# The bias of attention is added by TensorE, and maximum and exponentials read PSUM

## The chip, the cores and the metric

The kernel runs on one core of one Trainium2 chip. The metric is device time in microseconds (us), the median of several executions; one further execution is profiled. All data is float32.

## The reference

It is a network on one sequence of 256 tokens and width 1024. Four layers follow each other, each a feed-forward block, an attention block and a feed-forward block; their attention kinds are A, B, C, A. Then come a hybrid block H (attention beside a state-space scan) and a mixture of experts. Cut to what the change touches, each attention computes, per head and block of 128 queries:

```python
s = einsum("bqgrd,bkgd->bgrqk", q, k) * scale + bias      # H: no bias
s = where(ok, s, -1e30)
m = max(s);  m = maximum(m, sink)                         # sink: A only
e = exp(s - m)
denom = sum(e) + exp(sink - m)                            # sink: A only
o = einsum(e / denom, v)
```

The bias is a table of relative distances, one value per head and distance. Head width is 64, so the scale is 1/8. A looks back over a window of 128, B has three branches (compressed keys, selected blocks, window) mixed by gates, C is plain causal attention over the blocks chosen, which at this length are all.

## The kernel before, in words

Feed-forward blocks and projections stream weights through a ring of three slots in SBUF; they aren't touched. Each attention block is a list of units (`units_of`): for each half `a` of the queries (128 tokens) and each quad of four heads one unit, in B three (two scored branches `s` = 0 and 1, then one that only takes the compressed probabilities, `s` = 2). A, C have 8 scored units each, B 16 and 8 compressed ones, H 4. The number of keys `nk` is 128 for the first half of the queries (short units) and 256 for the second (long units); in H it is always 256.

A scored unit goes through these steps, each on one engine, joined by counting semaphores:

- scores, TensorE, L1197: four products over 64 rows into two banks of PSUM. Two pairs of banks are used in turn, by `i % 2`. The products alternate between array rows 0 to 63 and 64 to 127 (`half`).
- the biased pass, VectorE, `biased(i)`, L1283 to L1292: PSUM times 1/8 plus bias (in long units of A two pieces, one from the window table), written to the SBUF tile `scores` or `scores_more`, four of them in turn (`RINGS`). It ends with semaphore `sbias`, which frees the banks: the scores of unit i + 2 wait for it.
- the maximum, VectorE, L1296: a reduction over the SBUF tile, in A two small operations with the sink (L1298, L1300), and the negation L1301, which ends with `smax`.
- the exponentials, ScalarE, L1356: four activations, in place in SBUF, each with the row sum; ends with `sexp`.
- the coefficients, VectorE, L1309 to L1318: two or three small operations, end with `coef`.
- the scaling, GpSimd, L1388: the tile of four heads times the coefficients; ends with `psc`.
- the transposes, TensorE, L1216 (L1211 for a compressed unit): four or eight of 128x128, into banks 4 and 5.
- the copy to SBUF, ScalarE, L1371.
- the values, TensorE, L1237 (L1243 in C, L1233 compressed), and at the end of a query group a copy to `oT` on VectorE, L1322.

Each engine runs its own list in the order written. With `AHEAD = 3` TensorE runs the scores of units 0 to 2, then for each unit `scores(i + 3)`, `transposes(i)`, `values(i - 1)`. VectorE runs `biased` of 0 to 2, then for each unit `coefficients(i)`, `biased(i + 3)`, in H then a part of a convolution (L1698), and the copy out. ScalarE runs the exponentials of 0 and 1, then for each unit those of i + 2 and the copy of i. Before the first attention block the bias tables are put in order by products with a reversed identity (L1431) that ends at `cst[:, C_REV:...]`; after that this region isn't used.

Of the kernel before, what the change touches and what calls it, by code (L numbers as in the profile page):

```python
# [16 lines left out]
ALU = mybir.AluOpType  # L17
# [20 lines left out]
SLOT = 3 * KT * PAIR  # L38
RSQRT_MAGIC = 0x5F3759DF
RINGS = 4  # L40
AHEAD = 3

N_CMP = 15
CMP_STRIDE = 16
# [101 lines left out]
class Semaphores:  # L146


    def __init__(self, nc, ctx):
        def some(names):  # L150
            return [ctx.enter_context(nc.semaphore(n)) for n in names.split()]


        self.raw0, self.raw1, self.raw2, self.slots_used = \
            some("raw0 raw1 raw2 slots_used")

        self.gain0, self.gain1, self.x_in, self.consts_in = \
            some("gain0 gain1 x_in consts_in")

        self.bias_rows_in, self.bias_tab, self.bias_ps, self.bias_sum, self.bias_rows_out, self.bias_in = \  # L160
            some("bias_rows_in bias_tab bias_ps bias_sum bias_rows_out bias_in")
        self.bias_product, self.bias_turned, self.sinks_in = \
            some("bias_product bias_turned sinks_in")

        self.mean_sq, self.power = some("mean_sq power")

        self.ss_done, self.xs_ready, self.tr_done, self.hT_act, self.hT_dve, self.y_done = \
            some("ss_done xs_ready tr_done hT_act hT_dve y_done")
        self.post_used, = some("post_used")

        self.gu_hi, self.dn_hi, self.gu_lo, self.dn_lo, self.gu_done, self.silu = \
            some("gu_hi dn_hi gu_lo dn_lo gu_done silu")
        self.sgc, self.hid_done, self.hid_hi, self.hid_lo, self.down_done = \
            some("sgc hid_done hid_hi hid_lo down_done")

        self.proj, self.evac_act, self.evac_dve = \
            some("proj evac_act evac_dve")

        self.scores, self.sbias, self.smax, self.sexp, self.coef, self.psc = \
            some("scores sbias smax sexp coef psc")  # L180
        self.pT, self.pT_sb, self.oPV, self.oT_sb = \
            some("pT pT_sb oPV oT_sb")

        self.bgate, self.cmp_small, self.z2, self.chid_ps, self.gelu, self.chidT_ps = \
            some("bgate cmp_small z2 chid_ps gelu chidT_ps")
        self.chidT, self.kcb_ps, self.kcb, self.s_cmp, self.cmp_arg, self.cmp_exp = \
            some("chidT kcb_ps kcb s_cmp cmp_arg cmp_exp")
        self.pc, = some("pc")

        self.h_rows, self.h_small, self.h_sq, self.h_rope, self.h_qk_ps, self.h_qT = \  # L190
            some("h_rows h_small h_sq h_rope h_qk_ps h_qT")
        self.h_kT, self.h_ao, self.h_merge1, self.h_conv, self.h_silu, self.h_dtarg = \
            some("h_kT h_ao h_merge1 h_conv h_silu h_dtarg")
        self.h_dtexp, self.h_dta, self.h_acol_ps, self.h_cb_ps, self.h_xt_ps, self.h_row = \
            some("h_dtexp h_dta h_acol_ps h_cb_ps h_xt_ps h_row")
        self.h_arg, self.h_exp, self.h_y, self.h_yss, self.h_yn, self.h_yT_ps = \
            some("h_arg h_exp h_y h_yss h_yn h_yT_ps")
        self.h_yT, self.h_so, self.h_merge2, self.h_mT_ps, self.h_mT, self.h_zs = \
            some("h_yT h_so h_merge2 h_mT_ps h_mT h_zs")
        self.h_w_sum, = some("h_w_sum")  # L200

        self.e_small, self.e_hT, self.e_lg, self.e_arg, self.e_exp, self.e_comb = \
            some("e_small e_hT e_lg e_arg e_exp e_comb")
        self.e_rows, self.e_act, self.comb = \
            some("e_rows e_act comb")

        self.chain_act, self.chain_dve, self.out_done = \
            some("chain_act chain_dve out_done")


class Program:
# [10 lines left out]
    def map_memory(self):  # L222
# [140 lines left out]
        assert self.top <= 229344, self.top  # L363
        self.psum = self.ctx.enter_context(nc.psum_tensor("psum_all", [P, 8, 512], F32))
        self.ident = self.cst[:, C_ID:C_ID + P]
        self.one = self.cst[:, C_ONE:C_ONE + 1]
        self.minus_half = self.cst[:, C_MHALF:C_MHALF + 1]
        self.scratch = nc.dram_tensor("bias_rows", (2, NH, DTOEP), F32, kind="Internal").ap()
# [816 lines left out]
def pe_attention(K, pe, b):  # L1185
# [4 lines left out]
    def scores(i):  # L1190
        x = scored[i]
        if i >= 2:
            pe.wait_ge(K.sem.sbias, S0 + i - 1)
        for t in range(2):
            for half in range(2):
                hs = slice(half * HD, (half + 1) * HD)
                ins = nc.tensor.matmul(K.psum[:, 2 * (i % 2) + half, t * SEQ:t * SEQ + x["nk"]],  # L1197
                                       K.qT[hs, 2 * x["quad"] + t, x["a"] * P:(x["a"] + 1) * P],
                                       K.kT[hs, att.ktile(x["quad"], t, x["s"]), 0:x["nk"]],
                                       start=True, stop=True)  # L1200
        ins.then_inc(K.sem.scores, 1)

    def transposes(x):
# [47 lines left out]
    if kind == "H":  # L1251
        pe.wait_ge(K.sem.h_qT, 1)
        pe.wait_ge(K.sem.h_kT, 1)
    for i in range(AHEAD):
        scores(i)
    for x in b["units"]:
        if x["si"] is not None and x["si"] + AHEAD < len(scored):
            scores(x["si"] + AHEAD)
        transposes(x)
        if x["u"]:  # L1260
            values(b["units"][x["u"] - 1])
# [3 lines left out]
def dve_attention(K, dve, b):  # L1265
# [4 lines left out]
    def head_slice(x):  # L1270
        return slice(4 * x["quad"], 4 * x["quad"] + 4)

    def biased(i):

        x = scored[i]
        nk, hs = x["nk"], head_slice(x)
        src = K.psum[:, 2 * (i % 2):2 * (i % 2) + 2, :].rearrange("p b (h k) -> p (b h) k", h=2)[:, :, 0:nk]
        dst = K.S(i)[:, :, 0:nk]
        dve.wait_ge(K.sem.scores, S0 + i + 1)
        if i >= RINGS:  # L1280
            dve.wait_ge(K.sem.pT, U0 + scored[i - RINGS]["u"] + 1)
        if kind == "H":
            nc.vector.tensor_scalar(dst, src, SCALE, None, ALU.mult).then_inc(K.sem.sbias, 1)  # L1283
        elif kind == "A" and x["a"] == 1:

            nc.vector.scalar_tensor_tensor(out=dst[:, :, 0:P], in0=src[:, :, 0:P], scalar=SCALE,
                                           in1=K.biasA[:, hs, :], op0=ALU.mult, op1=ALU.add)
            nc.vector.scalar_tensor_tensor(out=dst[:, :, P:], in0=src[:, :, P:], scalar=SCALE,
                                           in1=K.bias[:, hs, P:], op0=ALU.mult, op1=ALU.add)\
                .then_inc(K.sem.sbias, 1)  # L1290
        else:
            nc.vector.scalar_tensor_tensor(out=dst, in0=src, scalar=SCALE, in1=K.bias[:, hs, SEQ - nk:],  # L1292
                                           op0=ALU.mult, op1=ALU.add).then_inc(K.sem.sbias, 1)
        dve.wait_ge(K.sem.sbias, S0 + i + 1)
        m = K.am[:, i % RINGS, :]
        K.link(dve, "dve", nc.vector.tensor_reduce(out=m, in_=dst, axis=AX, op=ALU.max))  # L1296
        if kind == "A":
            K.link(dve, "dve", nc.vector.tensor_tensor(m, m, K.sink[:, b["j"], hs], ALU.max))  # L1298

            K.link(dve, "dve", nc.vector.tensor_tensor(K.se[:, i % RINGS, :], K.sink[:, b["j"], hs], m, ALU.subtract))  # L1300
        nc.vector.tensor_scalar(m, m, -1.0, None, ALU.mult).then_inc(K.sem.smax, 1)  # L1301

    def coefficients(i):

# [20 lines left out]

    if kind == "B":
        dve.wait_ge(K.sem.bgate, 1)
    if kind != "H":
        dve.wait_ge(K.sem.bias_turned, len(bias_chunks(K)))
    for i in range(AHEAD):  # L1330
        biased(i)
    for x in b["units"]:
        if x["si"] is not None:
            coefficients(x["si"])
            if x["si"] + AHEAD < len(scored):
                biased(x["si"] + AHEAD)
            if kind == "H":
                dve_conv(K, dve, b, range(2 * x["si"], min(2 * x["si"] + 2, CONV_K)))
        if x["u"] >= 2 and b["units"][x["u"] - 2]["last"]:
# [6 lines left out]
def act_attention(K, act, b):  # L1346
# [4 lines left out]
    def exps(i):  # L1351
        x = scored[i]
        act.wait_ge(K.sem.smax, S0 + i + 1)
        for r in range(4):
            s = K.S(i)[:, r, 0:x["nk"]]
            ins = nc.scalar.activation(s, s, ACT.Exp, bias=K.am[:, i % RINGS, r:r + 1],  # L1356
                                       accum_out=K.den[:, i % RINGS, r:r + 1])
        if kind == "A":
            ins = nc.scalar.activation(K.se[:, i % RINGS, :], K.se[:, i % RINGS, :], ACT.Exp)
        ins.then_inc(K.sem.sexp, 1)  # L1360
# [10 lines left out]
            ins = nc.scalar.activation(K.PT[:, u % 2, 0:nj, :], K.psum[:, 4:4 + nj, :], ACT.Copy)  # L1371
        ins.then_inc(K.sem.pT_sb, 1)

    for i in range(AHEAD - 1):
        exps(i)
    for x in b["units"]:
        if x["si"] is not None and x["si"] + AHEAD - 1 < len(scored):
            exps(x["si"] + AHEAD - 1)
        copy_pT(x)


# [54 lines left out]
def act_bias(K, act, b):  # L1436
    for i, chunk in enumerate(bias_chunks(K)):
        act.wait_ge(K.sem.bias_product, i + 1)
        K.nc.scalar.activation(chunk, K.psum[:, 4 + i % 4, :], ACT.Copy).then_inc(K.sem.bias_turned, 1)


CMP_BANKS = (5, 6, 7, 4)
# [758 lines left out]
```

## Time and profile before

| | us |
|---|---|
| median of 3 runs (3224.70 to 3226.69) | 3224.71 |
| the profiled execution, its own time | 3223.67 |
| its span, first to last instruction | 3221.9 |
| TensorE busy, matmuls | 2902.3 (90%) |
| VectorE busy | 1449.7 (45%) |
| ScalarE busy | 1068.1 (33%) |
| GpSimd busy | 301.4 (9%) |

The page of the profile gives busy time of each engine, the granted clock of TensorE (mean 0.942 of full), and the chain of work that ended last, followed back from the last instruction. The five attention stretches run from the first scores of a block to the first product of its output projection. A product of float32 shows as two records on TensorE, a transpose as one.

### The profile page before, as it was taken

The page shows a single profiled execution, that of the slowest core. Times are in us where ns is not written, and L with a number is a line of the kernel's source. Part 1 is how long each engine was busy: PE and PEld are TensorE (multiplying, and loading weights), DVE is VectorE, ACT ScalarE, POOL GpSimd, SP SyncE. Part 2 cuts the span into 40 slices and gives each one's busy share as a digit, 9 for nine tenths or more (in the row PEclk, how much of TensorE's full clock was granted, in tenths as well). Part 3 has the DMA queues.
Part 4 walks back from the last instruction along what each step waited for, and adds up shares of the span by engine and source line. Part 5 has one row for each costly group of instructions (what it writes and reads, how often), then busy time and mean ns, then how long its engine had stood idle before and what let it go on. Part 6 is the DMA issues. An engine that isn't in the chain of part 4 may idle for free.

```text
span 3221.9 us, 45596 instructions
## 1 busy us (share of the span) xinstructions
PE 2902.3 (90%) x17916; PEld 2489.9 (77%) x17916; DVE 1449.7 (45%) x1815; ACT 1068.1 (33%) x1425; POOL 301.4 (9%) x444
## 2 busy tenths in 40 slices
PE   6988898998878989988898998799895669999999
PEld 5985698997746989975698997399653439999998
DVE  4443445552254454523455552545206525555554
ACT  3334333331163333313333332434103104333333
POOL 0011001001020010001001001100200000000000
PEclk9999999999889999999999999999997779999999
DMA  7532445452404544433454452345331033455442
GB/s 271 195 117 92 161 174 187 170 182 96 170 1 170 195 169 168 171 118 118 170 181 177 164 182 98 138 158 187 105 134 44 27 126 139 175 194 195 173 178 91
DMA packets 330150, 480.06 MB, mean 149 GB/s; under 512 B 9009, under 2 KB 266289, under 8 KB 330081
## 3 DMA queue, kind: packets, MB, share of 16 engines
q1 hardware_dynamic: 320640, 459.73, 40.0%
q0 software_dynamic: 4992, 16.08, 1.5%
q10 hardware_dynamic: 4448, 3.31, 0.3%
q8 instruction: 45, 0.74, 0.1%
q14 instruction: 25, 0.20, 0.0%
HBM read 478.00 MB, written 1.10 MB: 149 GB/s over the span
## 4 chain that ended last, share of the span: by engine, by line
PE 86%; DVE 8%; ACT 2%; POOL 2%; issue 1%; DMA 1%; ACTq 0%; DVEq 0%; PEldq 0%; POOLq 0%
PE psum_all L1030 15%; PE psum_all L1032 14%; PE psum_all L1031 14%; PE psum_all L1044 7%; PE psum_all L1045 7%; PE psum_all L1046 7%; PE psum_all L1091 6%; PE psum_all L1102 5%; PE psum_all L1406 4%; PE psum_all L726 1%; DVE attn_max L1296 1%; PE psum_all L1667 1%; PE psum_all L1216 1%; PE psum_all L1237 1%; PE psum_all L1197 1%
## 5 line engine op out<-in xcount | busy, mean ns | idle before, releaser
L1030 PE MATMUL psum_all<-hT_hi,gu_hi 128*128 128x256 f32 x3840 | 1095.6, 285 | 26.7 <-DVE hT_lo L752 17.2
L1032 PE MATMUL psum_all<-hT_hi,gu_lo 128*128 128x256 f32 x3840 | 1095.7, 285 | 0.0
L1031 PE MATMUL psum_all<-hT_lo,gu_hi 128*128 128x256 f32 x3840 | 1095.5, 285 | 0.0
L1030 PEld LDWEIGHTS psum_all<-hT_hi,gu_hi 128*128 128x128 f32 x3840 | 745.3, 194 | 38.2 <-issue 23.8
L1031 PEld LDWEIGHTS psum_all<-hT_lo,gu_hi 128*128 128x128 f32 x3840 | 745.2, 194 | 8.5
L1032 PEld LDWEIGHTS psum_all<-hT_hi,gu_lo 128*128 128x128 f32 x3840 | 744.9, 194 | 0.0
L841 DVE TENSOR_TENSOR gu_lo<-raw_ring,gu_hi 128x2048 fp32r<-128x2048 f32 x240 | 549.6, 2290 | 59.6 <-ACT gu_hi L829 59.6
L829 ACT ACTIVATE gu_hi<-raw_ring 128x2048 fp32r (+1 forms) x240 | 459.1, 1913 | 6.9 <-DVE oT L1322 6.9
L893 ACT ACTIVATE silu_gate<-psum_all 128x256 f32<-128x256 f32 x240 | 92.1, 384 | 1102.4 <-PE psum_all L1032 1102.4
L1044 PE MATMUL psum_all<-down_hi,hidden_hi 128*128 128x512 f32 x960 | 377.1, 393 | 0.0
L1045 PE MATMUL psum_all<-down_lo,hidden_hi 128*128 128x512 f32 x960 | 376.7, 392 | 0.0
L1046 PE MATMUL psum_all<-down_hi,hidden_lo 128*128 128x512 f32 x960 | 373.9, 390 | 0.0
L948 DVE TENSOR_TENSOR hidden<-silu_gate,psum_all 128x256 f32<-128x256 f32 x240 | 101.2, 422 | 566.4 <-ACT silu_gate L893 564.2
L1007 POOL TENSOR_TENSOR hidden_hi<-hidden,consts_sb 128x256 fp32r<-128x256 f32 x240 | 147.1, 613 | 1945.1 <-DVE hidden L948 1945.1
L836 ACT ACTIVATE down_hi<-raw_ring 128x1024 fp32r (+1 forms) x240 | 254.4, 1060 | 173.3 <-PE psum_all L1046 173.3
L848 DVE TENSOR_TENSOR down_lo<-raw_ring,down_hi 128x1024 fp32r<-128x1024 f32 x240 | 292.6, 1219 | 16.0 <-ACT down_hi L836 16.0
L1091 PE MATMUL psum_all<-hT,raw_ring 128*128 128x256 f32 x896 | 206.1, 392 | 8.5 <-PE psum_all L1091 4.5
L1046 PEld LDWEIGHTS psum_all<-down_hi,hidden_lo 128*128 128x128 f32 x960 | 180.7, 188 | 39.1
L1091 PEld LDWEIGHTS psum_all<-hT,raw_ring 128*128 128x128 f32 x896 | 175.5, 198 | 39.6 <-issue 10.7
L1044 PEld LDWEIGHTS psum_all<-down_hi,hidden_hi 128*128 128x128 f32 x960 | 181.4, 189 | 31.5 <-issue 0.4
L1045 PEld LDWEIGHTS psum_all<-down_lo,hidden_hi 128*128 128x128 f32 x960 | 181.4, 189 | 28.6
L953 DVE TENSOR_TENSOR hidden_lo<-hidden,hidden_hi 128x256 fp32r<-128x256 f32 x240 | 102.1, 425 | 191.3 <-POOL hidden_hi L1007 191.3
(280 smaller groups left out, 1947.6 us busy)
## 6 DMA issues: line engine op xcount, KB each, us to landing
raw_ring<-in_ffn_w_in SPq DMA_DIRECT2D x176, 1024.0 KB, 7.0
raw_ring<-in_w SPq DMA_DIRECT2D x96, 1024.0 KB, 7.4
raw_ring<-in_ffn_w_out SPq DMA_DIRECT2D x88, 1024.0 KB, 9.3
gain<-in_norm_g POOLq DMA_DIRECT2D x24, 512.0 KB, 4.4
raw_ring<-in_c_w_in SPq DMA_DIRECT2D x12, 768.0 KB, 5.2
raw_ring<-in_w_in SPq DMA_DIRECT2D x10, 768.0 KB, 5.8
raw_ring<-in_a_w_in SPq DMA_DIRECT2D x8, 768.0 KB, 5.1
raw_ring<-in_b_w_in SPq DMA_DIRECT2D x8, 768.0 KB, 5.1
```

The costliest lines, as they stand in the source:

```text
L829: K.nc.scalar.activation(K.gu_hi[:, t, :, :], raw_gu(K, slot, t), ACT.Copy).then_inc(K.sem.gu_hi, 1)
L836: K.nc.scalar.activation(K.dn_hi[:, t, :], raw_dn(K, slot, t), ACT.Copy).then_inc(K.sem.dn_hi, 1)
L841: K.nc.vector.tensor_tensor(K.gu_lo[:, t, :, :], raw_gu(K, slot, t), K.gu_hi[:, t, :, :].bitcast(F32), ALU.subtract).then_inc(K.sem.gu_lo, 1)
L848: K.nc.vector.tensor_tensor(K.dn_lo[:, t, :], raw_dn(K, slot, t), K.dn_hi[:, t, :].bitcast(F32), ALU.subtract).then_inc(K.sem.dn_lo, 1)
L1030: nc.tensor.matmul(out, w_hi, K.hT_hi[:, k, :], start=k == 0, stop=False)
L1031: nc.tensor.matmul(out, w_hi, K.hT_lo[:, k, :], start=False, stop=False)
L1032: ins = nc.tensor.matmul(out, w_lo, K.hT_hi[:, k, :], start=False, stop=k == KT - 1)
L1044: nc.tensor.matmul(out, h_hi, d_hi, start=first, stop=False)
L1045: nc.tensor.matmul(out, h_hi, d_lo, start=False, stop=False)
L1046: ins = nc.tensor.matmul(out, h_lo, d_hi, start=False, stop=last)
L1091: ins = nc.tensor.matmul(K.psum[:, bank, 0:SEQ], w[:, k, it["c0"]:it["c0"] + P], K.hT[:, k, :], start=k == 0, stop=k == KT - 1)
L1102: ins = nc.tensor.matmul(K.psum[:, bank, 0:it["n"]], K.hT[:, k, a * P:(a + 1) * P], w[:, k, it["c0"]:it["c0"] + it["n"]], start=k == 0 and ...
```

## The change

The biased pass goes. The scaled identity 8 x I is made once by a ScalarE copy over the reversed identity (semaphore `eight_id`). TensorE adds the bias as the first product of each bank's accumulation, 8 x I times the bias table, and the scores accumulate on it, so that PSUM holds the unscaled scores plus 8 x bias. The products are ordered by half: bias (two pieces in long units of A), then the two score products of this half. The maximum reduces PSUM; in A the scale comes in the operation with the sink, else in the negation. The exponentials read PSUM, with the scale as the activation's factor, and write the SBUF tile. The banks are now free when the exponentials have ended: scores wait for `sexp`. Work is issued two units ahead, and VectorE runs `maxima(i + 2)` before `coefficients(i)`. H has no bias product.

```diff
 def scores(i):
         x = scored[i]
         if i >= 2:
-            pe.wait_ge(K.sem.sbias, S0 + i - 1)
-        for t in range(2):
-            for half in range(2):
-                hs = slice(half * HD, (half + 1) * HD)
-                ins = nc.tensor.matmul(K.psum[:, 2 * (i % 2) + half, t * SEQ:t * SEQ + x["nk"]],
+            pe.wait_ge(K.sem.sexp, S0 + i - 1)
+        nk = x["nk"]
+        for half in range(2):
+            hs = slice(half * HD, (half + 1) * HD)
+            bank = K.psum[:, 2 * (i % 2) + half, :].rearrange("p (t k) -> p t k", t=2)
+            h0 = 4 * x["quad"] + 2 * half
+            if kind == "A" and x["a"] == 1:
+                nc.tensor.matmul(bank[:, :, 0:P], K.eight, K.biasA[:, h0:h0 + 2, :], start=True, stop=False)
+                nc.tensor.matmul(bank[:, :, P:], K.eight, K.bias[:, h0:h0 + 2, P:], start=False, stop=False)
+            elif kind != "H":
+                nc.tensor.matmul(bank[:, :, 0:nk], K.eight, K.bias[:, h0:h0 + 2, SEQ - nk:], start=True, stop=False)
+            for t in range(2):
+                ins = nc.tensor.matmul(bank[:, t, 0:nk],
                                        K.qT[hs, 2 * x["quad"] + t, x["a"] * P:(x["a"] + 1) * P],
-                                       K.kT[hs, att.ktile(x["quad"], t, x["s"]), 0:x["nk"]],
-                                       start=True, stop=True)
+                                       K.kT[hs, att.ktile(x["quad"], t, x["s"]), 0:nk],
+                                       start=kind == "H", stop=kind == "H" or t == 1)
...
-    for i in range(AHEAD):
+    if kind != "H":
+        pe.wait_ge(K.sem.eight_id, 1)
+    for i in range(2):
         scores(i)
     for x in b["units"]:
-        if x["si"] is not None and x["si"] + AHEAD < len(scored):
-            scores(x["si"] + AHEAD)
+        if x["si"] is not None and x["si"] + 2 < len(scored):
+            scores(x["si"] + 2)
         transposes(x)
...
-        dst = K.S(i)[:, :, 0:nk]
         dve.wait_ge(K.sem.scores, S0 + i + 1)
-        if i >= RINGS:
-            dve.wait_ge(K.sem.pT, U0 + scored[i - RINGS]["u"] + 1)
...
-            nc.vector.scalar_tensor_tensor(out=dst, in0=src, scalar=SCALE, in1=K.bias[:, hs, SEQ - nk:],
-                                           op0=ALU.mult, op1=ALU.add).then_inc(K.sem.sbias, 1)
-        dve.wait_ge(K.sem.sbias, S0 + i + 1)
         m = K.am[:, i % RINGS, :]
-        K.link(dve, "dve", nc.vector.tensor_reduce(out=m, in_=dst, axis=AX, op=ALU.max))
+        K.link(dve, "dve", nc.vector.tensor_reduce(out=m, in_=src, axis=AX, op=ALU.max))
...
-    for i in range(AHEAD):
-        biased(i)
+    for i in range(2):
+        maxima(i)
     for x in b["units"]:
         if x["si"] is not None:
+            if x["si"] + 2 < len(scored):
+                maxima(x["si"] + 2)
             coefficients(x["si"])
-            if x["si"] + AHEAD < len(scored):
-                biased(x["si"] + AHEAD)
...
         act.wait_ge(K.sem.smax, S0 + i + 1)
+        if i >= RINGS:
+            act.wait_ge(K.sem.pT, U0 + scored[i - RINGS]["u"] + 1)
         for r in range(4):
-            s = K.S(i)[:, r, 0:x["nk"]]
-            ins = nc.scalar.activation(s, s, ACT.Exp, bias=K.am[:, i % RINGS, r:r + 1],
-                                       accum_out=K.den[:, i % RINGS, r:r + 1])
+            nk = x["nk"]
+            src = K.psum[:, 2 * (i % 2) + r // 2, (r % 2) * SEQ:(r % 2) * SEQ + nk]
+            ins = nc.scalar.activation(K.S(i)[:, r, 0:nk], src, ACT.Exp, bias=K.am[:, i % RINGS, r:r + 1],
+                                       scale=SCALE, accum_out=K.den[:, i % RINGS, r:r + 1])
...
+    K.nc.scalar.activation(K.eight, K.ident, ACT.Copy, scale=1.0 / SCALE).then_inc(K.sem.eight_id, 1)
```

## Rows read from the trace of the kernel before

**Rows 1.** The page: the chain that ended last, shares by engine.
```profile
PE 86%; DVE 8%; ACT 2%; POOL 2%; issue 1%; DMA 1%; ACTq 0%; DVEq 0%; PEldq 0%; POOLq 0%
```

**Rows 2.** Table by stretch (A, B, C, A, H): length, busy (instructions), clock, DMA share, GB/s.
```profile
287.12:326.55 39.43, 24.29 (x161) 14.88 (x161) 26.27 (x76) 23.17 (x82) 11.72 (x8) 0.83 0.00 1
883.42:962.33 78.91, 60.73 (x385) 35.82 (x385) 45.22 (x104) 46.12 (x153) 23.44 (x16) 0.81 0.00 1
1496.56:1531.38 34.82, 23.61 (x208) 17.87 (x208) 22.17 (x48) 20.95 (x73) 11.73 (x8) 0.90 0.25 92
2016.09:2053.73 37.64, 22.63 (x160) 13.91 (x160) 26.80 (x76) 23.16 (x82) 11.72 (x8) 0.91 0.24 84
2448.43:2487.72 39.29, 21.52 (x96) 14.29 (x96) 33.58 (x69) 15.79 (x43) 8.01 (x4) 0.60 0.00 0
```

**Rows 3.** The chain in order of time, block B: start, us, engine, tile, line.
```profile
935.51 1.90 POOL scores_more L1388
...
937.46 1.97 PE psum_all L1216 x8
939.43 1.71 PE psum_all L1237 x8
941.14 0.54 PE psum_all L1211 x4
941.68 1.02 PE psum_all L1237 x8
942.70 1.09 PE psum_all L1197 x8
...
943.81 1.24 DVE scores_more L1292
...
945.07 1.23 DVE attn_max L1296
...
947.06 1.90 POOL scores L1388
```

**Rows 4.** Timeline of the first A: start, us, engine, line, operation, tiles [idle <-releaser].
```profile
288.69 0.69 DVE L1296 TENSOR_REDUCE attn_max<-scores 128x4 f32<-128x512 f32 x1
...
302.32 1.04 POOL L1388 TENSOR_TENSOR scores_more<-scores_more,attn_coef 128x512 f32<-128x512 f32 x1 [4.55 <-DVE attn_coef L1318]
...
303.47 1.22 DVE L1296 TENSOR_REDUCE attn_max<-scores 128x4 f32<-128x1024 f32 x1
...
307.33 1.22 DVE L1296 TENSOR_REDUCE attn_max<-scores_more 128x4 f32<-128x1024 f32 x1
...
308.97 0.17 DVE L1301 TENSOR_SCALAR attn_max<-attn_max 128x4 f32<-128x4 f32 x1
...
309.69 0.49 ACT L1356 ACTIVATE scores_more<-scores_more,attn_max 128x256 f32<-128x256 f32 x1
```

**Rows 5.** Groups by line, biased passes: busy us, mean ns | idle before, releaser.
```profile
L1292 DVE SCALAR_TENSOR_TENSOR scores<-psum_all,bias_full 128x512 f32<-128x512 f32 (+1 forms) x16 | 14.2, 888 | 31.6 <-PE psum_all L1197 31.5
...
L1286 DVE SCALAR_TENSOR_TENSOR scores<-psum_all,bias_window 128x512 f32<-128x512 f32 x4 | 2.7, 683 | 3.9 <-PE psum_all L1197 3.9
```

**Rows 6.** TensorE prices: two lines of the chain, then four of the timeline.
```profile
275.87 10.58 PE psum_all L1431 x24
...
789.10 14.07 PE psum_all L1091 x64
...
303.42 0.66 PE L1216 MATMUL psum_all<-consts_sb,scores_more 128*128 128x128 f32 x4 [2.33 <-POOL scores_more L1388]
304.00 0.65 PE L1237 MATMUL psum_all<-probsT,v_tok 128*64 128x256 f32 x4
...
942.63 1.14 PE L1197 MATMUL psum_all<-kT,qT 64*128 64x256 f32 x8
943.70 1.09 PE L1216 MATMUL psum_all<-consts_sb,scores 128*128 128x128 f32 x8
```

**Rows 7.** The chain in order of time, block H: a part of the convolution.
```profile
2465.79 6.36 DVE h_xbcT L1698 x12
```

**Rows 8.** Timeline, first A: the scores of the first long unit.
```profile
296.50 2.08 PE L1197 MATMUL psum_all<-kT,qT 64*128 64x256 f32 x8
```

More of the change, by code:

```diff
@@ L40 @@
 RINGS = 4
-AHEAD = 3
 N_CMP = 15
@@ L177, in __init__ @@
             some("proj evac_act evac_dve")
-        self.scores, self.sbias, self.smax, self.sexp, self.coef, self.psc = \
-            some("scores sbias smax sexp coef psc")
+        self.scores, self.eight_id, self.smax, self.sexp, self.coef, self.psc = \
+            some("scores eight_id smax sexp coef psc")
         self.pT, self.pT_sb, self.oPV, self.oT_sb = \
@@ L365, in map_memory @@
         self.ident = self.cst[:, C_ID:C_ID + P]
+        self.eight = self.cst[:, C_REV:C_REV + P]
         self.one = self.cst[:, C_ONE:C_ONE + 1]
@@ L1271, in head_slice, with maxima @@
         return slice(4 * x["quad"], 4 * x["quad"] + 4)
-    def biased(i):
+    def maxima(i):
         x = scored[i]
@@ L1277, in biased @@
         src = K.psum[:, 2 * (i % 2):2 * (i % 2) + 2, :].rearrange("p b (h k) -> p (b h) k", h=2)[:, :, 0:nk]
-        dst = K.S(i)[:, :, 0:nk]
         dve.wait_ge(K.sem.scores, S0 + i + 1)
-        if i >= RINGS:
-            dve.wait_ge(K.sem.pT, U0 + scored[i - RINGS]["u"] + 1)
[L1282 to L1291, printed above, removed]
-            nc.vector.scalar_tensor_tensor(out=dst, in0=src, scalar=SCALE, in1=K.bias[:, hs, SEQ - nk:],
-                                           op0=ALU.mult, op1=ALU.add).then_inc(K.sem.sbias, 1)
-        dve.wait_ge(K.sem.sbias, S0 + i + 1)
         m = K.am[:, i % RINGS, :]
-        K.link(dve, "dve", nc.vector.tensor_reduce(out=m, in_=dst, axis=AX, op=ALU.max))
+        K.link(dve, "dve", nc.vector.tensor_reduce(out=m, in_=src, axis=AX, op=ALU.max))
         if kind == "A":
-            K.link(dve, "dve", nc.vector.tensor_tensor(m, m, K.sink[:, b["j"], hs], ALU.max))
+            K.link(dve, "dve", nc.vector.scalar_tensor_tensor(out=m, in0=m, scalar=SCALE, in1=K.sink[:, b["j"], hs],
+                                                              op0=ALU.mult, op1=ALU.max))
             K.link(dve, "dve", nc.vector.tensor_tensor(K.se[:, i % RINGS, :], K.sink[:, b["j"], hs], m, ALU.subtract))
-        nc.vector.tensor_scalar(m, m, -1.0, None, ALU.mult).then_inc(K.sem.smax, 1)
+        nc.vector.tensor_scalar(m, m, -1.0 if kind == "A" else -SCALE, None, ALU.mult).then_inc(K.sem.smax, 1)
     def coefficients(i):
@@ L1327, in dve_attention @@
         dve.wait_ge(K.sem.bgate, 1)
-    if kind != "H":
-        dve.wait_ge(K.sem.bias_turned, len(bias_chunks(K)))
-    for i in range(AHEAD):
-        biased(i)
+    for i in range(2):
+        maxima(i)
     for x in b["units"]:
         if x["si"] is not None:
+            if x["si"] + 2 < len(scored):
+                maxima(x["si"] + 2)
             coefficients(x["si"])
-            if x["si"] + AHEAD < len(scored):
-                biased(x["si"] + AHEAD)
             if kind == "H":
@@ L1372, in copy_pT @@
         ins.then_inc(K.sem.pT_sb, 1)
-    for i in range(AHEAD - 1):
+    for i in range(2):
         exps(i)
     for x in b["units"]:
-        if x["si"] is not None and x["si"] + AHEAD - 1 < len(scored):
-            exps(x["si"] + AHEAD - 1)
+        if x["si"] is not None and x["si"] + 2 < len(scored):
+            exps(x["si"] + 2)
         copy_pT(x)
```

## The prediction

> **What bounds the kernel now.** I read first the chain of work that ended last: TensorE is 86% of it, VectorE 8% [rows 1]. The table by stretch then gives the five attention stretches, which are all that the change touches: 230.1 us together, with TensorE busy for 152.8, VectorE for 154.0, ScalarE for 129.2 and GpSimd for 66.6 [rows 2]. No engine fills them; they are bound by a chain from engine to engine, and the question is which links it has after the change. Call a unit's steps S (scores), b (the biased pass), M (maximum and its small operations), E (exponentials), C (coefficients), G (GpSimd's scaling), T (transposes) and V (values). In block B the chain goes round once per pair of scored units: G 1.90, T 1.97, V 1.71, the transposes of the compressed unit 0.54, V 1.02, S 1.09, b 1.24, M 1.43, C 0.66, in all 11.55 us from G to G [rows 3]. So GpSimd's scaling is in the loop already, because TensorE's queue runs S(i+3) ahead of T(i), but behind T(i-1). In A, VectorE sets the pace of the long units: one long reduction starts 3.86 us after the one before [rows 4].
>
> **Removed.** The b passes: two groups of 14.2 and 14.1 us, four of 2.7 and two of 2.4, 43.9 us of VectorE [rows 5] (one row stands there for the two first groups, one for the four of 2.7). It is the most that can be saved.
>
> **Moved, and this is the point on which I forecast.** Work was issued three units ahead, now two. TensorE's queue is S0, S1, then S(i+2), T(i), V(i-1) for each unit; VectorE's is M0, M1, then M(i+2) before C(i). Follow it: M(k) must end before C(k-2) starts; then G(k-2), then T(k-2), V(k-3), and only behind these, in TensorE's order, S(k+1), which M(k+1) waits for. Every maximum thus hangs on the one before by C, G, T, V, S and M in series: one round per unit, where before there was one per pair. The new wait of S(i) for the exponentials of i-2 comes due earlier than the wait behind T (E of a long unit is 4 x 0.49 + 0.19 = 2.2 us [rows 4], while C, G and T take 3.7), so it costs only at a block's start. The wait for pT in front of the exponentials looks four units back and costs nothing. The number of maximum-to-maximum rounds beyond the first three maxima is 5 in each A, 5 in C, 13 in B.
>
> **S itself.** Before, the two halves of the array work side by side: a long S takes 1.14 [rows 6]. Now each half is: bias product over all 128 rows, then two products on 64 rows, then the same for the other half; the full-array product between them separates the halves. A 512-column f32 record takes 10.58/24 = 0.44 and each product has two; a 256-column one 14.07/64 = 0.22; eight 128-column records take 1.09, less a tail of 0.2, so 0.11 each [rows 6]. Long: 4 x 0.43 + 8 x 0.215 = 3.45; short: 4 x 0.22 + 8 x 0.11 = 1.73. Going from one shape of the array to another costs some 0.2: the S of 942.63 needs four pairs of records, 0.87, and the next T starts after 1.07 [rows 6]. Three such changes more, 0.6, and a tail of 0.16 give 4.2 and 2.5. Bounds: 3.4 with no change costing anything, 4.8 with 0.4 for each. The Trainium skill, "TensorEngine Tiling (Array Packing)", Key Properties, says that changing the tiling mode drains the engine; it gives no time. The 0.2 agrees with it, and the rule speaks against this change; the sum rests on the row.
>
> **The other links.** M: long in A, from 307.33 to the end of the last small operation at 309.14, 1.82 [rows 4]; in B and C 1.43 [rows 3]; short 0.53 less, as the short reduction takes 0.69 against 1.22 [rows 4]. The reduction now reads PSUM: b, which read the same 1024 elements out of PSUM, took 1.24 [rows 3], so I add nothing (0 to 0.1 each). C: three small operations in A and B, two in C and H, at 0.2 each like those of M, so 0.58 and 0.38. G with its two hand-overs: 2.0 long, 1.15 short [rows 3, 4]. T and V long take 1.05 and 1.02, start to start [rows 3, 6], short 0.58 each (T's start to V's [rows 6], V taken to be the same). The exponentials out of PSUM lie beside this chain (0 to 0.1 each way). The scaled identity is one ScalarE copy, 0.2 once.
>
> **Sum, with TensorE at its full clock.** A round in A: short 6.7; short with a long S and M behind it 8.9; long 0.57 + 2.0 + 1.05 + 1.02 + 4.2 + 1.85 = 10.7. A from the first S: M2 ends at 9.6 (S0 2.7, M0 1.3, E0 1.75, S2 2.5, M2 1.3), then 6.1, 8.9, 8.9, 8.9, 10.3, so the last maximum ends at 52.8; then a tail of 11.9 (C5, G5, T5, V4, a copy, C7, G7, T7, copy, V7, copy). In all 64.7, against 39.4 and 37.6 [rows 2]: +25.3 and +27.1. C: M2 ends at 8.4, then 5.5, 8.4, 8.4, 8.4, 9.8, a tail of 12.4 (its V has sixteen records of half the length, and I give it 0.5 more): 61.2 against 34.8: +26.4. B has two kinds of round. Out of a first unit: C, G, T, the compressed V 0.5, S, M: 9.8 long, 6.2 short. Out of a second one T must be copied (1.1) before the compressed transposes (0.54) and V can go: 12.0 long, 7.6 short. With 8.4 at the start, 27.6 for two short pairs, 6.2 + 9.85 + 8.45 + 9.85 across the change of length, 2 x 21.8, 9.8 and a tail of 13.5: 137.3 against 78.9: +58.4. H has no bias, its queue of VectorE is full of convolution (rounds of 6.36 us) [rows 7], and S stays at 1.1. It loses its four b, 4.8, and gains a stall in front of M2, which waits for E0 2.2 and S2 1.2 while M1 takes 1.43: 2.0. So H gives -2.8. Together +134.4 us.
>
> **TensorE's clock.** Right after G, with TensorE idle before it, T came at half clock (1.97 for eight records against 1.09 behind S), V in part (1.71 against 1.02), and a long S once (2.08 against 1.14) [rows 3, 6, 8]; the granted clock of the attention stretches is 0.81 to 0.91 but for H's 0.60 [rows 2]. Now TensorE stands idle in each round for M, C and G, 4.4 us if long and 2.7 to 3.0 if short, longer than before the T at 937.46, whose G alone took 1.9. T and V at half cost 0.9 and up to 0.9 more; the head of S sometimes comes with them. I take 2.0 per round: 28 x 2.0 = 56. The tails of before had such stretches in them and mine don't: 4 x 1.5 = 6; B begins behind long vector work, so its first S at half: 2.5. Together +64.5. Bounds: 0, and all of TensorE's work in these rounds at half, about +134. The Trainium skill, "TensorE: Matmul & The Clock Gate", HAM oscillation, says that idle gaps between bursts of matmuls bring the clock down and each burst then starts slow; the rows agree.
>
> 3223.7 (the profiled execution; its span 3221.9; the median of the runs is 1.0 higher) + 134.4 + 64.5 = 3422.6, so 3423. DMA and the feed-forward blocks keep their times: in the first A and in B the DMA share during attention is 0.00, so a longer stretch there delays no transfer and hides none [rows 2].
>
> **Rivals.** (1) The rounds as above, but TensorE is not slowed: its S, now longer, keeps the clock up: 3223.7 + 134.4 = 3358. For it: T behind S took 1.09 [rows 6]. Against: T behind G took 1.97 [rows 3], and in the new order T is always behind G. (2) The clock stays at half through nearly all: 3223.7 + 134.4 + 134 = 3492; H does so already, at 0.60 [rows 2]. (3) S is cheap, since the halves still overlap and the bias record of one half slips beside the products of the other: S 2.2 and 1.4 instead of 4.2 and 2.5: 28 rounds at 1.6 less, and about half as much again where they would have run at half clock, 68 in all: 3355. (4) Faster: VectorE is the bound as in A's 3.86 us, and the loop over G doesn't close. Then the 43.9 us of b go and the pace of a long unit is that of ScalarE, whose 2.2 us of E and about 1.0 of copy lie under the 3.86 of today: 3223.7 - 43.9 = 3180. It decides if S(k+1) can be worked before T(k-2) ends; TensorE's queue is in order and T stands before it, and B's chain goes through G today, so this needs my reading of the order to be wrong. (5) The two effects cancel and nothing can be measured: 3224.
>
> **How the numbers follow.** My case 0.70, between 3370 and 3475; (1) 0.09, (2) 0.11, (3) 0.05, (4) 0.03, (5) 0.02. The likeliest gives 3423. The range 3355 to 3485 takes in my case, (1) and (3) and leaves out (2), (4) and (5), 0.16. Faster by over 0.2% (about what a measurement of this kernel can tell from no change) 0.03, within 0.2% 0.02, slower 0.95.
>
> **What would show it.** In the chain of waits of the changed kernel, B must show C, G, T, V, S, M once per unit and no b; the starts of long reductions in A should be 10.7 us apart or more, in B about 10 and 12 in turn. A long S should span near 4 us at full clock. Stretches: A 76, B 167, C 73, H 37. VectorE's busy time should be 44 us lower and its idle time far higher, waiting for the scores. TensorE's granted clock should be lower in A, B and C. It would be wrong if starts of reductions lie closer than E + S + M, or if T comes at full clock after each G.

## The result, and the profile after

The changed kernel takes 3443.8 us (median, 3440.5 to 3445.4), the kernel before 3225.3; the ratio is 1.0675, 95% interval 1.0657 to 1.0694. The profiled execution has a span of 3440.6 us, 218.7 more than before. From the page of the changed kernel, the engines, then the chain that ended last:

```profile
PE 3067.4 (89%) x18108; PEld 2574.9 (75%) x18108; DVE 1411.4 (41%) x1763; ACT 1064.2 (31%) x1426; POOL 301.4 (9%) x444
...
PE 87%; DVE 7%; POOL 2%; ACT 2%; DMA 1%; issue 1%; SPq 0%; DVEq 0%; PEldq 0%; ACTq 0%
```

The table by stretch of the changed kernel, bounds as in [rows 2] (A, B, C, A, H): length, busy time of TensorE, its weight loads, VectorE, ScalarE, GpSimd, then granted clock, DMA share, GB/s.

```profile
290.33:367.97 77.64, 53.86 (x208) 32.80 (x208) 19.40 (x64) 22.25 (x81) 11.72 (x8) 0.76 0.00 0
924.51:1109.13 184.62, 137.74 (x448) 71.14 (x448) 30.56 (x88) 45.13 (x152) 23.44 (x16) 0.63 0.00 0
1643.42:1715.03 71.61, 52.91 (x240) 32.81 (x240) 15.54 (x41) 20.22 (x72) 11.72 (x8) 0.81 0.12 45
2200.46:2276.03 75.57, 51.78 (x208) 31.79 (x208) 19.42 (x64) 22.32 (x82) 11.72 (x8) 0.80 0.12 42
2670.49:2707.51 37.02, 20.54 (x96) 14.23 (x96) 30.46 (x65) 14.04 (x40) 8.01 (x4) 0.71 0.00 1
```

The five lengths sum to 446.5 us against 230.1: +216.4, so all but 2 us of the loss is here. VectorE is busy 38.7 us less (115.4 against 154.0), as meant. TensorE is busy for 164 us more, and in A, B and C its clock is lower (in H it is higher, 0.71 for 0.60). The two largest groups of S in the changed kernel: bias products (L1203; those of A's long units, L1200 and L1201, stand apart) and score products (L1205), busy us, mean ns, and idle time before them.

```profile
L1205 PE MATMUL psum_all<-kT,qT 64*128 64x256 f32 (+1 forms) x352 | 100.4, 439 | 3.6 <-DVE kT L1641 1.9 <-ACT scores L1352 1.7
L1203 PE MATMUL psum_all<-bias_full,consts_sb 128*128 128x256 f32 (+1 forms) x128 | 75.0, 678 | 8.7 <-DVE cmp_probs L1504 5.6 <-ACT consts_sb L1436 1.0 <-ACT attn_sink_exp L1355 1.0
```

And the group that waits: before its 44 maxima VectorE stood idle for 303.6 us, waiting for the scores. Before the change it was the biased passes that waited for them, 48.2 us in all their groups together, 31.6 of them in the group of [rows 5].

```profile
L1290 DVE TENSOR_REDUCE attn_max<-psum_all 128x4 f32<-128x1024 f32 (+1 forms) x44 | 43.2, 982 | 303.6 <-PE psum_all L1205 303.6
```

The chain in order of time through a query group of long units in B, which answers to [rows 3]: start, us, engine, tile, line (L1384 is GpSimd's scaling, L1224 transposes, L1241 and L1245 values, L1219 compressed transposes, L1290 the maximum).

```profile
1042.29 0.96 PE psum_all L1219 x4
1043.26 1.10 PE psum_all L1245 x8
1044.35 1.06 PE psum_all L1203 x2
1045.41 1.06 PE psum_all L1205 x4
1046.47 1.05 PE psum_all L1203 x2
1047.52 1.07 PE psum_all L1205 x4
...
1048.62 1.24 DVE attn_max L1290
...
1050.61 1.90 POOL scores_more L1384
...
1052.56 1.97 PE psum_all L1224 x8
1054.53 1.05 PE psum_all L1241 x4
1055.58 2.01 PE psum_all L1203 x2
1057.58 2.00 PE psum_all L1205 x4
1059.59 2.00 PE psum_all L1203 x2
1061.59 2.02 PE psum_all L1205 x4
...
1063.63 1.24 DVE attn_max L1290
...
1065.62 1.90 POOL scores_more L1384
```

Two things can be seen. The chain goes round once per scored unit, from G at 1050.61 to G at 1065.62, 15.0 us; in [rows 3] it was 11.55 for two units. And S takes 4.24 us the first time (four pieces of 1.06) and 8.03 the second (four of 2.0): the same instructions at full and at half clock (2.4 and 1.2 GHz).

### The profile page after: what moved, and what is told of

Read it like the earlier page. It is cut to its first block, busy times and chain, and to the rows that moved or that the text cites. A ratio compares the mean times of both kernels' runs of the same rounds, so it can differ in the third digit from the quotient of the medians.

```text
span 3440.6 us, 45928 instructions
## 1 busy us (share of the span) xinstructions
PE 3067.4 (89%) x18108; PEld 2574.9 (75%) x18108; DVE 1411.4 (41%) x1763; ACT 1064.2 (31%) x1426; POOL 301.4 (9%) x444
## 4 chain that ended last, share of the span: by engine, by line
PE 87%; DVE 7%; POOL 2%; ACT 2%; DMA 1%; issue 1%; SPq 0%; DVEq 0%; PEldq 0%; ACTq 0%
PE psum_all L1030 14%; PE psum_all L1031 14%; PE psum_all L1032 14%; PE psum_all L1044 6%; PE psum_all L1045 6%; PE psum_all L1046 6%; PE psum_all L1091 6%; PE psum_all L1102 4%; PE psum_all L1402 4%; PE psum_all L1205 3%; PE psum_all L1203 2%; PE psum_all L1224 2%; PE psum_all L726 1%; DVE attn_max L1290 1%; PE psum_all L1245 1%
## 5 line engine op out<-in xcount | busy, mean ns | idle before, releaser
L1046 PEld LDWEIGHTS psum_all<-down_hi,hidden_lo 128*128 128x128 f32 x960 | 180.3, 188 | 39.3
```

Source lines behind the costliest of these rows:

```text
L1046: ins = nc.tensor.matmul(out, h_lo, d_hi, start=False, stop=last)
```

## The experiments

Three causes had to be told apart: the order and the number of units ahead; the bias products with their longer S; and the clock. The times are those of each kernel against the kernel before on the same chip (3224.4 to 3225.3).

**The order alone, put into the kernel before.** Bias and scores stay as they were.

```diff
-AHEAD = 3
+AHEAD = 2
...
-            coefficients(x["si"])
             if x["si"] + AHEAD < len(scored):
                 biased(x["si"] + AHEAD)
+            coefficients(x["si"])
```

(ScalarE's exponentials keep their two units ahead.)

> The kernel before with nothing but the order of the change: two units ahead on TensorE and VectorE, the biased pass and maximum of unit i + 2 in front of the coefficients of unit i. Bias stays on VectorE, scores stay short. Theory (the order alone closes the loop once per unit): as the changed kernel without bias products (3331) plus the biased pass in 28 rounds, 1.25 us long or 0.7 short, so 3355 to 3370, with A near 62 and B near 139. Rival (the order only hurts together with banks held until the exponentials end): within 20 us of 3225.

Measured 3362.3 us, ratio 1.043 (1.0413 to 1.0448). Its two first stretches, A and B:

```profile
287.36:350.27 62.91, 30.17 (x160) 18.33 (x160) 26.91 (x76) 23.65 (x82) 11.72 (x8) 0.67 0.00 0
907.29:1045.59 138.30, 75.90 (x384) 43.87 (x384) 45.56 (x105) 47.22 (x152) 23.44 (x16) 0.63 0.00 0
```

62.9 and 138.3, where 62 and 139 were expected. The order and the units ahead cost 137 us by themselves. This is shown, and the rival, that it only hurts with banks held longer, is out. Part of the 137 is clock: it is 0.67 and 0.63 here, where [rows 2] has 0.83 and 0.81. The two, one unit less ahead and the maximum before the coefficients, were not tried apart in this kernel; in the changed one, the second alone is worth 131 us (two kernels further down).

**The changed kernel without bias products.** Bias and mask are left out; the scores are those of the kernel before.

> The changed kernel without the bias products, so bias and mask are left out; the score products alternate between the halves as before the change. It tells the price of the bias on TensorE from that of the order. Theory of the prediction: 20 long rounds lose 3.06 us each and 8 short ones 1.8, 75 us, and with the half clock some 110, so about 3335, which leaves some 110 us over the kernel before to the order alone. Rival (the bias products are all of it): within 20 us of 3225.

Measured 3331.4, ratio 1.033 (1.0312 to 1.0349): near the 3335 expected. So the loss splits, by edits and with what each does to the clock: order and units ahead +137.0 (3225.3 to 3362.3), the biased pass gone from it -30.9 (3362.3 to 3331.4), the bias products and the order of the halves +112.4 (3331.4 to 3443.8). The middle figure also holds the change to banks freed by the exponentials. VectorE's saving is thus real, 31 of its 44 us, and it is bought with 112.

**The changed kernel with the old order on VectorE.** Two units ahead stay, as do the bias products.

```diff
+            coefficients(x["si"])
             if x["si"] + 2 < len(scored):
                 maxima(x["si"] + 2)
-            coefficients(x["si"])
```

> The changed kernel, but VectorE runs the coefficients of unit i before the maximum of unit i + 2. Theory (the order closes a loop once per unit): coefficients and GpSimd's scaling no longer wait for the maximum of two units later, the loop goes round once per two units, and TensorE's own work of 6.3 us per long and 3.7 us per short unit sets the pace. Attention stretches near 50 (A), 100 (B), 50 (C), 37 (H) instead of 78, 185, 72, 37, so about 3280 in all. Rival (the longer scores on TensorE are the cause, the order hardly matters): the time stays within 30 us of 3444.

Measured 3313.2, ratio 1.0276 (1.0257 to 1.0294): 131 us back for two calls exchanged. The expectation of 3280 was 33 too low: B alone took 49 us more than expected, the others a little less. Its A, B and C, and then a part of its B by itself:

```profile
287.99:334.29 46.30, 41.59 (x208) 25.97 (x208) 18.31 (x64) 21.70 (x82) 11.74 (x8) 0.96 0.00 0
891.20:1039.98 148.78, 137.59 (x448) 70.53 (x448) 28.08 (x88) 43.68 (x152) 23.46 (x16) 0.62 0.00 1
1575.93:1621.70 45.77, 43.12 (x240) 27.45 (x240) 14.52 (x41) 19.60 (x72) 11.74 (x8) 0.96 0.20 70
...
937.00:985.00 48.00, 45.20 (x110) 20.30 (x108) 8.38 (x27) 12.82 (x47) 6.91 (x5) 0.50 0.00 1
```

A and C took 46 where I expected 50. In those 48.0 us of B TensorE was busy for 45.2 and had half its clock all the time. The clock is low at the start of B, where TensorE has waited for VectorE's long work, but hardly a gap is left that could keep it there: another reason was wanted, and the next three kernels look for it. The low clock did end in this block, at about 999.5, behind a stretch in which TensorE had run transposes and values and no scores (start, us, engine, tile, line):

```profile
997.09 1.91 PE psum_all L1245 x8
999.00 1.54 PE psum_all L1203 x2
1000.54 1.06 PE psum_all L1205 x4
```

**The changed kernel with the halves side by side again.** Both bias products first, then the score products alternating.

```diff
-            for t in range(2):
-                ins = nc.tensor.matmul(bank[:, t, 0:nk],
+        for t in range(2):
+            for half in range(2):
...
+                ins = nc.tensor.matmul(banks[half][:, t, 0:nk],
```

> The changed kernel, but both bias products of a unit come first and then the four score products, alternating between the two halves of the array as before the change. Work and idle gap of a round stay, the scores of a long unit should take 2.95 instead of 4.2 us, of a short one 1.6 instead of 2.5 (at full clock). By that alone 28 rounds are 1.1 us shorter, about -31 us, to 3413. Theory on the clock (products that fill only half the array's rows let the clock fall or stay low): the granted clock in B rises from 0.63 to over 0.70 and the gain is 50 to 80 us. Rival on the clock (only TensorE's idle share counts): less work beside the same idle gap, so the clock in B is no higher than 0.63 and the gain is at most 45 us.

> The kernel with the halves alternating and the order of the change once more, for its profile: 3392 us was measured for it, 51 less than the changed kernel. Theory (half-filled products keep the clock low): the granted clock in B is over 0.70 against 0.63 of the changed kernel. Rival (idle share only): 0.63 or lower, and the gain comes from the shorter scores at half clock.

Measured 3392.3, ratio 1.0513 (1.0495 to 1.0532), 51 us less than the changed kernel, and 3393.2 in a single further run, from which this row of B comes:

```profile
916.16:1071.26 155.10, 108.10 (x448) 56.45 (x448) 30.40 (x89) 45.20 (x152) 23.43 (x16) 0.72 0.00 1
```

TensorE has less to do in each round beside the same idle gap, and yet its clock is higher, 0.72 against 0.63. The idle share alone doesn't explain this. In the other blocks it went the other way: the clock was 0.73 in the first A (0.76 in the changed kernel), 0.79 in C (0.81) and 0.77 in the second A (0.80), as the rival on the clock would have it. And in B, too, an S behind T and V still ran at half clock as a whole, 3.71 and 1.83 us where the next one took 1.91 and 1.09:

```profile
999.32 3.71 PE psum_all L1203 x4
1003.03 1.83 PE psum_all L1207 x8
...
1015.23 1.91 PE psum_all L1203 x4
1017.14 1.09 PE psum_all L1207 x8
```

**Both edits.**

> Both edits at once: VectorE runs coefficients before the maximum, and the score products alternate between the halves behind the two bias products. The kernel with the order alone took 3313, with its B stretch at 148.8 us and a granted clock of 0.62 although TensorE was busy for 137.6 of them. Theory on the clock (score products on half the array at a time don't bring a low clock back up): with the halves side by side the clock in B comes to over 0.85, TensorE needs 5.0 us per long unit and 2.8 per short one, stretches 42, 90, 42, 42, 37 and 3240 to 3250 in all. Rival (the clock in B stays low for another reason, as the block begins at half clock): clock in B at 0.65 or lower, B near 125, the whole near 3280.

Measured 3250.3, ratio 1.0079 (1.0062 to 1.0096). Its A and B:

```profile
288.71:328.94 40.23, 33.40 (x208) 22.20 (x208) 18.49 (x64) 21.59 (x81) 11.72 (x8) 0.96 0.00 0
885.42:983.14 97.72, 80.21 (x448) 43.81 (x448) 28.19 (x88) 43.66 (x152) 23.45 (x16) 0.92 0.00 1
```

B goes from 148.8 to 97.7 us by the order of each unit's products alone, its clock from 0.62 to 0.92. The block begins at half clock here too, so that isn't enough to hold it down. The edit does two things at once: it puts the two bias products one behind the other, and it alternates the halves. Which of them lets the clock come back was not tried.

**A warmed start of B.** The kernel with only VectorE's order undone (3313), with eight useless full-array products of 512 columns on TensorE while it waits before the first scores of B.

> The kernel with the order alone undone, and eight useless full-array products of 512 columns on TensorE while it waits before the first scores of B, nothing else. In that kernel B began at half clock and stayed there (0.62, 148.8 us) while A and C, which begin at full clock, kept 0.96 with the same products. Theory (score products on half the array keep a full clock but don't bring back a low one, so it is how the block starts): B stays near full clock, over 0.85, takes 98 to 110 us, and the whole about 3265 to 3275. Rival (something in B itself, its compressed units or their waits, holds the clock down): B stays above 140 us and the whole near 3313.

Measured 3282.2, ratio 1.018 (1.0165 to 1.0196), and B:

```profile
895.43:1006.11 110.68, 94.00 (x450) 49.74 (x448) 28.23 (x88) 43.76 (x153) 23.47 (x16) 0.95 0.00 1
```

The same instructions take 110.7 us instead of 148.8 when the block starts at full clock: the rival, something in B itself, is out. The stretch is at the upper end of the expectation and the whole 7 us above it, in part because B now begins about 4 us later (895.43 for 891.20), behind the useless products. With the run before, this is what the rows show: in the order bias, half, bias, half a full clock is mostly kept, and a low one lasts long, even with hardly a gap. It is no rule without exceptions. In the kernel with VectorE's order undone the clock came back at about 999.5, and in the first A of the changed kernel it came back in the middle of an S, at about 350.4. The eight products ahead of B had it back before the first S. What decides it in each case stays open.

Nor is it the order of the halves that keeps them apart. In H of the changed kernel the halves are written one after the other as well, but with no bias product between them, and the eight records take the 1.14 us of [rows 6]:

```profile
2676.19 1.14 PE L1205 MATMUL psum_all<-kT,qT 64*128 64x256 f32 x8 [1.65 <-ACT scores L1352]
```

So what separates the halves in A, B and C is the full-array product between them, as the prediction had it.

**The idle gap filled.** The changed kernel with useless full-array products between the scores of unit i + 2 and the wait for the scaled probabilities of unit i. They write bank 4, so the wait that frees it (`pT_sb`) now stands before them.

```diff
...
+            if kind != "H" and x["si"] + 2 < len(scored):
+                for _ in range(3 if x["nk"] == SEQ else 2):
+                    nc.tensor.matmul(K.psum[:, 4, :], K.ident, K.bias[:, 0:2, :].rearrange("p h s -> p (h s)"),
+                                     start=True, stop=True)
             pe.wait_ge(K.sem.psc, S0 + x["si"] + 1)
```

> The changed kernel with useless full-array products on TensorE between the scores of unit i + 2 and the wait for the scaled probabilities of unit i: three of 512 columns (2.6 us at full clock) in long units, two in short ones, in the time in which TensorE otherwise idles. Nothing that is needed waits for them at full clock. Theory (the idle gap of each round brings the clock down, and this costs 2 to 4 us a round): the granted clock in B rises from 0.63 to over 0.85, a long round falls from 13 to 15 us to about 11, and the whole takes 50 to 90 us less, near 3375. Rival (the clock doesn't follow the idle gap): rounds stay or grow by up to 1 us each, 3444 to 3475.

Measured 3367.7, ratio 1.0446 (1.0428 to 1.0465), 76 us less than the changed kernel, for more work on the engine that the chain goes through. A and B:

```profile
290.18:354.44 64.26, 53.62 (x236) 29.98 (x236) 19.36 (x64) 22.27 (x82) 11.72 (x8) 1.00 0.00 1
910.94:1058.59 147.65, 133.99 (x516) 66.15 (x516) 30.52 (x88) 45.13 (x152) 23.44 (x16) 0.91 0.00 1
```

A at full clock takes 64.26, and the prediction's sum at full clock had 64.7; C, at full clock too, takes 60.98, where the sum had 61.2. B, at 0.91, takes 147.7 where the sum at full clock had 137.3. So 76 of the 218 us come back with the clock, in spite of the added work.

**A cheaper bias product.** The kernel with both edits, with bias tables and scaled identity written as rounded float32; the bias is then rounded.

> As the kernel with both edits, and the bias tables and the scaled identity are written as rounded float32 (one record per product instead of two slower ones), so the bias is rounded. A long S then has 0.43 of bias products instead of 1.72 and takes 1.7 us, a short one 1.0. TensorE needs 3.8 us per long unit; the chain over two units (S, M, E, copy, T, V) 8.9, so 4.5 per long unit in A against 3.86 before the change, and about 10 per query group in B against 11.5. Theory: 3225 to 3240 in all, that is the edit of the change, cleared of its order and of the price of its products, at best equals the kernel before. Rival (VectorE's 44 us come through once the two are out of the way): 3200 or less.

Measured 3219.1, ratio 0.998 (0.997 to 0.999), a little under the expected 3225 to 3240, and the rival, 3200 or less, is out. A, B, C and the second A take 35.4, 84.2, 33.1 and 36.8 us, H 34.8. Only B is above [rows 2].

**Each block its own way.** As the last, but B keeps biased pass, order and three units ahead of the kernel before.

> The kernel with both edits and the rounded bias (3219.1), but block B keeps the biased pass, the order and the units ahead of the kernel before, with the rounded tables. That kernel's stretches against those before the change: A 35.4 for 39.4, C 33.1 for 34.8, second A 36.8 for 37.6, H 37 for 39, but B 84.2 for 78.9. Theory (the blocks don't touch each other): B returns to 79 and the whole is 3214, 0.3 to 0.4% under the kernel before. Rival (B's 5 us were the clock at its start, which is the same here): no less than 3218.

Measured 3212.7, ratio 0.9961 (0.9947 to 0.9975). It is faster than the kernel before by 0.4%, with an interval that stays below 1; the bias is rounded here too. Its stretches:

```profile
289.76:327.75 37.99, 29.95 (x184) 19.61 (x184) 18.41 (x64) 21.56 (x82) 11.72 (x8) 0.82 0.00 0
885.72:964.77 79.05, 60.86 (x384) 35.88 (x384) 45.11 (x105) 46.09 (x152) 23.44 (x16) 0.81 0.00 1
1499.17:1532.41 33.24, 27.39 (x224) 20.39 (x224) 14.08 (x41) 19.45 (x72) 11.72 (x8) 0.95 0.27 96
2018.45:2052.40 33.95, 24.47 (x184) 16.08 (x184) 18.33 (x64) 21.64 (x82) 11.72 (x8) 1.00 0.26 93
2445.69:2480.48 34.79, 21.64 (x96) 14.16 (x96) 27.81 (x65) 14.59 (x41) 7.86 (x4) 0.56 0.00 1
```

B is back at 79. The two A blocks run the same instructions and differ by 4.0 us with their clocks of 0.82 and 1.00. The gain of both A blocks together is 5.1 us (77.1 to 71.9), so a small edit can't be judged from one block alone. The gain of H, 39.3 to 34.8, needs no rounding, since H has no bias; a kernel with that alone was not run.

## Why the prediction was right, point by point

- **The round per unit.** It was forecast from the two queues, and the chain of B shows it: C, G, T, V, S, M with no b. With the order alone the kernel before loses 137 us.
- **S.** 4.2 us long at full clock; the four rows from 1044.35 to 1048.59 give 4.24. The changes of the array's shape at 0.2 are borne out piece by piece: each takes 1.06, where its records need 0.86 by the prediction's prices. The Trainium skill's rule ("TensorEngine Tiling (Array Packing)", Key Properties) that they drain the engine stands with it.
- **The stretches.** Forecast 76, 167, 73, 76 and 37; measured 77.6, 184.6, 71.6, 75.6 and 37.0. Four of five are within 2 us. In part this is luck: the clock went in as one estimate of 2.0 us for every round, and the rounds differ far more than that. The starts of long reductions lie 10.5 to 13.7 us apart in the first A and 12.4 to 15.0 in B, where 10.7 in A and about 10 and 12 in turn in B were the times at full clock.
- **What failed is the clock term in B.** I took 2.0 us per round, 26 for its 13 rounds, 2.5 for its start and 1.5 for its tail, 30 in all. B took 184.6 against my 137.3 at full clock, 47 in place of 30, and with that the whole came out 21 us above 3423. The step that was wrong is that only T, V and the head of S run at half. In B whole S's did: 8.03 for 4.24. The idle gap brings the clock down, as the filled gap shows, but I had it back too soon. This doesn't need the halves kept apart: in the kernel before with the order alone, an S behind T and V ran at half as a whole too, 2.03 for 1.09 [rows 3], and with the halves side by side behind the bias products one took 5.54 for 3.00.

```profile
1000.60 1.97 PE psum_all L1216 x8
1002.57 1.05 PE psum_all L1233 x4
1003.62 2.03 PE psum_all L1197 x8
```

  The longer S of the change has more to lose by it, and in B the clock stayed low through 11 us of unbroken TensorE work (1052.56 to 1063.61). The order of the products has a share in that, as the kernels with and without it show; it is no more than some 12 of the 47 us by an estimate: B was 29.5 us shorter with the halves side by side, and 17 of these are the shorter scores at full clock (8 x 1.25 + 8 x 0.9, by the times of that experiment's expectation). Rival (2), half clock through nearly all, described B better than my case (worked out from the terms of its bound, about 196), and A and C worse.
- **The bound of the clock.** The Trainium skill's account ("TensorE: Matmul & The Clock Gate", HAM oscillation) is that bursts parted by idle gaps each start slow. The trace agrees for the gap; the 48 us of the kernel with the old order at 0.50, with 45.2 of them busy, are no case of a gap.
- **VectorE.** It was forecast 44 us less busy and is 38.7 less over the five stretches. Of the other 5 us, 3.0 stand in three groups that grew: the first products of H's convolution (3.2 us for 1.7) and two small operations of the coefficients (10.5 for 9.7 and 5.7 for 5.0); the rest is not accounted for. With the order of the change, 31 us of the saving came through (3362.3 to 3331.4), because b was a link of every round there; the rounds of my sum hold no b, so they have this in them.
- **H.** -2.8 forecast, -2.3 measured. S stayed at 1.1 as I had it, and the stall of 2.0 is there: with VectorE's order undone (the kernel with the warmed start) H takes 35.1 instead of 37.0.
- **The faster rival** asked that S could be worked before T of an earlier unit. It can't in this queue; the same edits with the order undone and the products made cheap do gain, 0.2%, and 0.4% where B is left as it was.

## What to carry to other kernels

In a pipeline written out by hand over several engines, write down each queue and look for the loop through all of them: which step must end before the same step of the next unit can start, and once per how many units. Work moved off one engine gains nothing if the order puts one more link in series, and exchanging two calls can be worth more than the passes saved. Before TensorE is given work to relieve VectorE, price the products at both clocks, and let no full-array product come between products on the two halves of the array.

## What the runs showed of the hardware

I had not expected that the granted clock can stay at half while TensorE works almost without a gap. In the kernel with VectorE's order undone it was 0.50 over 48.0 us with TensorE busy for 45.2 of them, where each half's score products stood between full-array bias products; it came back in the same block some 15 us later. With the bias products together and the halves side by side the block had 0.92, and with the first order but started at full clock 0.95. The score products of a long unit, written half after half, took 1.14 us in H, no longer than when they alternate, and 2 x 1.06 with a bias product between the halves. Useless full-array products in TensorE's idle time made the changed kernel 76 us faster, and eight of them before one block another kernel 31 us (3313.2 to 3282.2).
